# Feed-forward of a two-layer streaming encoder: another order of the nine matmuls of a block

## The reference, cut to what matters

```python
def conv_ffn(h, conv_state, w_up, conv_w, conv_b, w_down):
    t = h.shape[1]
    u = h @ w_up                       # 1024 -> 2 x 2816
    up = jnp.concatenate([conv_state, u], axis=1)
    y = conv_b
    for j in range(CONV_W):            # causal convolution over tokens, width 3
        y = y + up[:, j:j + t] * conv_w[j]
    a, g = jnp.split(y, 2, axis=-1)
    return (jax.nn.silu(g) * a) @ w_down, up[:, -(CONV_W - 1):]
```

## Time and profile before

| | |
|---|---|
| Median of 3 runs | 3518.88 us (3518.0 to 3522.95) |
| The profiled execution's own time | 3523.37 us |
| Its span, first to last instruction | 3521.8 us |
| Mean granted clock of TensorE, share of full speed | 0.966 |
| TensorE busy | 3245.8 us (92%) |
| VectorE busy | 1852.8 us (53%) |
| ScalarE busy | 1198.1 us (34%) |
| GpSimd busy | 430.5 us (12%) |

### The profile page before, as it was taken

The page is one execution under the profiler, slowest core; times in us unless marked ns, Lnnn a source line. Parts: engine busy times, 40 slices in busy tenths (PEclk is TensorE's granted clock), DMA queues, the critical chain, the costliest instruction groups (busy, mean ns, idle before and its releaser), DMA issues. The chain is left out here.

```text
span 3521.8 us, 53106 instructions
## 1 busy us (share of the span) xinstructions
PE 3245.8 (92%) x20552; PEld 1867.0 (53%) x20758; DVE 1852.8 (53%) x3222; ACT 1198.1 (34%) x2527; POOL 430.5 (12%) x820
## 2 busy tenths in 40 slices
PE   7889886788999999999989999999989999999998
PEld 3555553454555555555445555555545555555555
DVE  4355555554655455555555555554646545555546
ACT  3355554433312222222235555553433222222221
POOL 1123322311000000000012222221110000000000
PEclk7899998899999999999989999999999999999999
DMA  9233321321322222232123444444421111111111
GB/s 358 78 100 105 105 83 46 119 78 42 110 66 70 63 60 60 69 92 66 49 90 119 133 133 132 132 134 134 135 67 44 37 48 42 42 42 37 42 43 61
DMA packets 247845, 305.16 MB, mean 87 GB/s; under 512 B 25027, under 2 KB 199607, under 8 KB 247042
## 3 DMA queue, kind: packets, MB, share of 16 engines
q1 hardware_dynamic: 217762, 191.78, 17.5%
q0 software_dynamic: 29920, 111.15, 10.5%
HBM read 265.99 MB, written 64.10 MB: 94 GB/s over the span
## 5 line engine op out<-in xcount | busy, mean ns | idle before, releaser
L96 PE MATMUL psum<-h,ffn_high 128*128 128x512 f32 (+1 forms) x2016 | 986.1, 529 | 2.8 <-ACT u L1069 2.8
L98 PE MATMUL psum<-hl,ffn_high 128*128 128x512 bf16 (+1 forms) x1933 | 587.3, 336 | 0.0
L100 PE MATMUL psum<-h,ffn_low 128*128 128x512 bf16 (+1 forms) x1973 | 552.6, 332 | 2.9
L96 PE MATMUL psum<-actr,ffn_high 128*128 128x512 f32 (+1 forms) x960 | 470.2, 530 | 7.3 <-DVE xT L672 7.3
L96 PEld LDWEIGHTS psum<-h,ffn_high 128*128 128x128 f32 x2016 | 390.1, 194 | 88.5 <-issue 8.9
L98 PEld LDWEIGHTS psum<-hl,ffn_high 128*128 128x128 bf16 x2016 | 196.7, 98 | 410.1 <-issue 353.0
L86 PE MATMUL psum<-h,attC_high 128*128 128x384 f32 (+2 forms) x768 | 362.3, 472 | 21.7 <-issue 8.3
L1142 DVE TENSOR_SCALAR y<-u,cvT 128x1168 f32<-128x1168 f32 x88 | 78.2, 888 | 540.5 <-ACT u L1074 540.4
L86 PE MATMUL psum<-h,attAB_high 128*128 128x384 f32 (+2 forms) x672 | 324.1, 482 | 19.0 <-DVE attAB_low L189 8.5
L98 PE MATMUL psum<-actl,ffn_high 128*128 128x512 bf16 (+1 forms) x921 | 280.8, 338 | 0.0
L1068 ACT COPY u<-psum 128x1024 f32<-128x1024 f32 x88 | 89.4, 1015 | 526.5 <-PE psum L100 526.0
(11 more groups left out here) (470 smaller groups left out, 6033.6 us busy)
## 6 DMA issues: line engine op xcount, KB each, us to landing
raws<-in_w_up SPq DMA_DIRECT2D x66, 512.0 KB, 4.0
ada_raw<-in_ada_w SPq DMA_DIRECT2D x24, 1024.0 KB, 9.4
m_raw<-in_ada_w SPq DMA_DIRECT2D x48, 512.0 KB, 7.3
raw_C<-in_cache_c_v POOLq DMA_DIRECT2D x64, 256.0 KB, 4.0
out_ck_s<-in_cache_c_k POOLq DMA_DIRECT2D x8, 1984.0 KB, 8.7
out_cv_s<-in_cache_c_v POOLq DMA_DIRECT2D x8, 1984.0 KB, 14.6
raws<-in_w_in_odd SPq DMA_DIRECT2D x24, 512.0 KB, 11.9
raw_C<-in_cache_c_k POOLq DMA_DIRECT2D x48, 256.0 KB, 5.5
```

The lines of the kernel that those rows point to most:

```text
L96: return pe.matmul(out, w, x[:, lo:hi], start=first and start, stop=last and stop, skip_group_check=True)
L98: return pe.matmul(out, top(w), xl[:, lo:hi], start=first and start, stop=last and stop, skip_group_check=True)
L100: return pe.matmul(out, wl, top(x[:, lo:hi]), start=first and start, stop=last and stop, skip_group_check=True)
```

## The change

The nine matmuls of a block are the same, each into the same bank and with the same operands; their order changes, and with it which one of a bank carries `start` and `stop`. Nothing outside `mm9` changes.

```diff
     one(0, "h", True, False)
-    one(0, "x", False, False)
+    one(1, "h", True, False)
     one(2, "h", True, False)
     one(2, "x", False, False)
     one(2, "w", False, True)
-    one(0, "w", False, True)
-    one(1, "h", True, False)
-    one(1, "x", False, False)
-    return one(1, "w", False, True)
+    one(0, "w", False, False)
+    one(1, "w", False, False)
+    one(1, "x", False, True)
+    return one(0, "x", False, True)
```

## The result

The changed kernel takes 3499.22 us as the median of four runs (3484.0 to 3503.31), the kernel before 3520.91 in the four runs beside it: a ratio of 0.9927 with a 95% interval of [0.9906, 0.9947]. It is faster by 0.73%, 22 us by the medians and 26 us by the ratio. A second measurement, six runs later on, gives 0.9931 [0.9918, 0.9944]. The forecast was 3467 us, a gain of 52 us: the direction holds, and the full range (3447 to 3524) has the time in it, but the forecast's own range (3449 to 3488) does not. **About half of the gain is missing.**

What follows compares the result with a forecast made beforehand. TensorE's feed-forward matmul stream was taken as the bound. Per-block extras 0.026 + 0.017 + 0.028 + 0.002 + 0.004 = 0.077 us, not 0.129, save 0.051 us x 1024 = 52 us: median 3467, own range 3449 to 3488, full 3447 to 3524.

Steps and rivals of the forecast that it cites:

- What bounds the kernel: Feed-forward: TensorE busy almost throughout on one stream of matmuls, so the time of a nine-matmul block sets the span.
- 0h to 1h and 1h to 2h: new: Between neighbouring four-byte high-weight matmuls, banks 0, 1, 2: load hidden, 0.002 us each; wrong if over 0.027 us.
- 2h to 2x: Bank 2, the block's one remaining change from four-byte to two-byte matmul: 0.026 us over columns.
- 2x to 2w: Bank 2, two-byte matmul right behind the change of type, its load also late: 0.017 us over columns.
- the split of the 0.129: Old block's 0.129 us beyond columns: nearly all put down to three four-byte-to-two-byte changes and the late loads behind them.
- 8 and 9: Profile rows on four-byte transposes and float32 multiplies, whose loads hide; taken as lower bound for neighbouring high-weight matmuls.
- The two-byte steps: Four steps per block between two-byte matmuls whose loads have had time: 0.007 us each, bounds 0.002 and 0.014.
- The load laid open: Rival: loads behind four-byte matmuls exposed whatever their type, 0.10 to 0.14 us for each of two; 3708 us; chance 0.20.
- The extra belongs to each h: Rival: some 0.025 us behind each four-byte high-weight matmul whatever follows; 6 us saved, 3513 us; chance 0.11.
- Another engine takes the gain: Rival: feed-forward waits of TensorE grow and take half the gain; 3493 us; chance 0.03.
- The change does not do what it says: Rival: assembler could drop loads of weights already there; only hidden loads would go, no time in them; no chance given.
- The page weighed there: Skill's rule that TensorE pulls weight loads ahead: by it alone the change is worth nothing; trace disagreed, 0.26 us idle.

## Why the size came out wrong

**What bounds the kernel** held. TensorE's feed-forward is one stream, the block is the unit, and the gain of 1024 blocks (29 us) is what the feed-forward got shorter by (28.4 us).

**The step that failed** is the one that reads "0h to 1h and 1h to 2h: new [...] I take 0.002 each, the lower end". They are 0.020 (0x to 1h, 447 ns against 427, which holds the step from 0x to 0h as well) and 0.023 us (1h to 2h, 236 against 213). The step named a condition of failure, "over 0.027 us" from h to h, that neither reaches; together with 0x to 0h they cost 0.037 more than was taken, and only 0.015 of that came back, where 2h to 2x is cheaper than its 0.026. Beside the forecast, over columns, in us a block:

| Step | forecast | measured in the changed kernel |
|---|---|---|
| 0x to 0h, 0h to 1h | 0.004 | 0.020 |
| 1h to 2h | 0.002 | 0.023 |
| 2h to 2x | 0.026 | 0.011 |
| 2x to 2w | 0.017 | 0.015 |
| 2w to 0w | 0.007 | 0.007 |
| 0w to 1w, 1w to 1x | 0.014 | 0.024 |
| 1x to 0x | 0.007 | 0.002 |
| sum | 0.077 | 0.102 |

(The measured steps are rounded medians; the block itself, 1.540 us, gives 0.100.)

**Behind it stands the split of the 0.129.** The prediction saw 0.025 to 0.03 us at every h followed by x and a late load of x in the same place, behind long h with the weight path idle for 0.26 us, and took the one for the price of the other. Two experiments part them. With one such change more the block takes 0.013 us more where the forecast's list charges 0.031 (1.553 against 1.540), and with the h in two bytes the two h that have an h behind them lose their excess as well (215 and 216 ns, block 1.484). The rest of the cost belonged to the h and w themselves: some 0.02 us for a long h, some 0.01 for a long w. The rows before could not part the two, since every h there is followed by a late load; but one gave a hint: ahead of 2x the weight path stands idle for 0.08 us only (1502.29 to 1502.37), and the excess there, 0.026, is about that of the long h. The rows for the lower bound, 8 and 9, were of multiplies at two ticks a column, another form than h, and what they show of fixed cost did not hold for it. Rows 9 stand, moreover, in a stretch with a granted clock of 0.51 (33 to 38 us), the lower level (1.2 GHz), where the feed-forward has the upper one; the prediction does not say so. That the form differs it noted, and took the rows all the same.

**The two-byte steps** were within bounds: 0.007 was right for 2w to 0w, too low by 0.005 for the two long w (their spaced operand, 226 and 225 ns, against 216 when dense), too high by as much for 1x to 0x, which is dense. The lower end of the forecast's range has a slip: with 0.002 for the three steps not seen the saving is 0.066 us a block (0.071 for all four) and not 0.068, 2 or 3 us in all; nothing hangs on it.

**The rivals.** *The load laid open* is refuted for this order: the loads of 1h and 2h start beneath the h before them, and h to h is nowhere near 0.10. Its mechanism exists, though, and shows once the cover is gone: a short h ahead of a long one costs 0.060 us a block and turns the gain into a loss. *The extra belongs to each h* was half right, and the measured block (1.540) lies in the middle between its 1.563 and the forecast's 1.517: it holds for the 0.02 us of a long h and fails for the part that goes with the change of type. *Another engine takes the gain* is refuted: TensorE's waits in the first feed-forward stretch are 1.1 us, and in the second, 2620 to 3400 us, 10.2 where they were 10.6. *The change does not do what it says* is refuted by 3072 loads and 3072 multiplies of line 96.

**The page weighed there.** By the rule on weight loads that are pulled ahead (the Trainium skill, "TensorE: Matmul & The Clock Gate", section "Step-by-step: what each phase is for") the change was by itself worth nothing; a gain of 0.73% disagrees, unless it is the change of type in the multiplies that costs and not the late load, which the runs do not part. The rows after show both sides of the rule: loads of h that run beneath the h before them, and in the order with two changes a two-byte load behind a long h that is not drawn forward, with 0.26 us of idle.

**Shown and open.** Shown: the gain comes from fewer changes between four-byte and two-byte multiplies, since it is zero without the four-byte type and one change alone is worth 0.013 us. Shown: spaced operands cost about 10 ns on 512 columns, by a swap of that operand alone, and by a dense copy with the same values. Not parted: whether a long h pays its 0.02 us for the moving operand or for four-byte weights, as both types were swapped together. Not parted either: whether a change of type costs its time by the late load of x or in the multiplies themselves, as the two always come together. Open too: why a w ahead of an h pays less than elsewhere.

## What to carry to other kernels

Where a stream of multiplies mixes four-byte and two-byte operands, put those of one type together and keep a long multiply ahead of every four-byte load; but credit such an order only with the changes that it removes, 0.013 to 0.020 us each here. Idle time on the weight path is no price by itself: find two neighbouring places that differ in it alone, or run the kernel in which they do, before the whole excess is put down to it. And the operand layout may be worth as much as the order: a dense copy of a spaced operand gave 0.027 us in each block that used it, as much as the reordering.

## What the runs showed of the hardware

At the clock's upper level (granted 0.99 to 1.00 in these stretches) a two-byte multiply with a dense moving operand follows its like after 216 ns at 512 columns and 56 at 128; with the operand's two bytes taken out of every four, after 225 to 226 and 60; a four-byte h of 512 columns with its load beneath another multiply takes 20 to 23 ns more than the 213 of its columns. And 0.26 us during which the weight path waits for nothing that the profile shows can go with a cost of no more than 13 ns.
